# One of four weight units of a pair formed on GpSimd instead of VectorE

## The reference

```python
xn   = rms_norm(h, norm_pre_mix);  cols = xn @ w_in
# cols -> q, k, v | r, k, v and four decay/rate parts, gate | two merge gates
o_attn = banded_gqa_attention(q, k, v, sink)
o_rwkv = rwkv7_bidirectional(...)      # 32 heads of 64, a forward and a backward scan
mix  = (sigmoid(g_attn) * o_attn + sigmoid(g_rwkv) * o_rwkv) @ w_out
h    = h + rms_norm(mix, norm_post_mix)
h    = h + rms_norm(square(relu(rms_norm(h, norm_pre_ffn) @ w_ffn_up)) @ w_ffn_down, norm_post_ffn)
```

## Time and profile before

| | us |
|---|---|
| median of 3 runs | 2259.21 |
| lowest and highest | 2257.98, 2265.47 |
| profiled execution | 2251.1 |
| its span | 2249.3 |
| TensorE busy | 2097.0 (93%) |
| VectorE busy | 1312.6 (58%) |
| ScalarE busy | 926.4 (41%) |
| GpSimd busy | 357.3 (16%) |
| mean granted TensorE clock | 0.962 of full |

### The profile page before, as it was taken

The page is one execution under the profiler, slowest core; times in us unless marked ns, Lnnn a source line. Parts: engine busy times, 40 slices in busy tenths (PEclk is TensorE's granted clock), DMA queues, the critical chain, the costliest instruction groups (busy, mean ns, idle before and its releaser), DMA issues.

```text
span 2249.3 us, 39352 instructions
## 1 busy us (share of the span) xinstructions
PE 2097.0 (93%) x14475; PEld 1912.1 (85%) x14475; DVE 1312.6 (58%) x2229; ACT 926.4 (41%) x1670; POOL 357.3 (16%) x424
## 2 busy tenths in 40 slices
PE   6999997999999999999999887979999999999996
PEld 6999996988888888888888766769989889899894
DVE  4666466566676666666666633455555555555554
ACT  4555333444444444434444422344434334344342
POOL 0000001333333333333333320000000000000000
PEclk9999998999999999999999857989999999999998
DMA  7546655223322322232331303535665656656662
GB/s 201 147 134 165 176 143 137 73 71 81 80 67 75 80 78 60 78 80 62 80 80 43 118 0 112 160 104 186 187 187 186 184 181 181 185 185 183 187 186 93
DMA packets 415085, 281.25 MB, mean 125 GB/s; under 512 B 14042, under 2 KB 372668, under 8 KB 414012
## 3 DMA queue, kind: packets, MB, share of 16 engines
q1 hardware_dynamic: 414620, 277.43, 42.7%
q10 hardware_dynamic: 416, 3.15, 0.4%
HBM read 278.46 MB, written 2.10 MB: 125 GB/s over the span
## 4 chain that ended last, share of the span: by engine, by line
issue 54%; PE 28%; DVE 10%; POOL 4%; ACT 2%; DMA 0%; SPq 0%; DVEq 0%; POOLq 0%; ACTq 0%
PE bank L1384 6%; PE bank L1386 5%; PE bank L1385 5%; POOL CT L1330 2%; DVE wlo L776 2%; PE bank L1639 2%; PE bank L1654 1%; PE bank L1400 1%; PE bank L1401 1%; PE bank L1402 1%; DVE dec L1027 1%; POOL st L1308 1%; PE bank L1659 1%; DVE kh L1019 1%; PE bank L1456 1%
## 5 line engine op out<-in xcount | busy, mean ns | idle before, releaser
L1384 PE MATMUL bank<-xT,whi 128*128 128x256 f32 x2784 | 820.4, 295 | 9.0 <-DVE wlo L776 4.6
L1385 PE MATMUL bank<-xT,whi 128*128 128x256 f32 x2784 | 787.2, 283 | 0.0
L1386 PE MATMUL bank<-xT,wlo 128*128 128x256 f32 x2784 | 786.8, 283 | 0.0
L1384 PEld LDWEIGHTS bank<-xT,whi 128*128 128x128 f32 x2784 | 533.6, 192 | 16.3 <-issue 10.1
L1385 PEld LDWEIGHTS bank<-xT,whi 128*128 128x128 f32 x2784 | 533.8, 192 | 1.5
L1386 PEld LDWEIGHTS bank<-xT,wlo 128*128 128x128 f32 x2784 | 532.2, 191 | 0.0
L776 DVE TENSOR_TENSOR wlo<-raw,whi 128x1024 fp32r<-128x1024 f32 (+1 forms) x160 | 244.1, 1525 | 164.1 <-ACT whi L424 102.7
L1262 DVE TENSOR_TENSOR wlo<-raw,whi 128x1024 fp32r<-128x1024 f32 x126 | 154.4, 1226 | 201.1 <-ACT whi L743 201.1
L743 ACT ACTIVATE whi<-raw 128x1024 fp32r<-128x1024 f32 x126 | 133.0, 1055 | 218.1 <-PE bank L1402 218.1
L1401 PE MATMUL bank<-wlo,ft 128*128 128x512 f32 x512 | 202.2, 395 | 0.0
L1402 PE MATMUL bank<-whi,ft 128*128 128x512 f32 x512 | 202.2, 395 | 0.0
(11 more groups left out here) (214 smaller groups left out, 3267.6 us busy)
## 6 DMA issues: line engine op xcount, KB each, us to landing
raw<-in_w_in SPq DMA_DIRECT2D x106, 1024.0 KB, 6.0
raw<-in_w_ffn_up SPq DMA_DIRECT2D x64, 1024.0 KB, 6.3
raw<-in_w_ffn_down SPq DMA_DIRECT2D x64, 1024.0 KB, 5.0
raw<-in_w_out SPq DMA_DIRECT2D x16, 1024.0 KB, 5.0
raw<-in_w_in SPq DMA_DIRECT2D x4, 768.0 KB, 4.7
xtok<-in_x SPq DMA_DIRECT2D x2, 1024.0 KB, 5.8
upg<-in_g_up SPq DMA_DIRECT2D x16, 128.0 KB, 3.4
hres<-in_x ACTq DMA_DIRECT2D x1, 2048.0 KB, 9.3
```

What stands on the lines that cost most here:

```text
L1384: M(bank[:, 0:T], h, xT[:, k, 0, :], start=k == 0, stop=False)
L1385: M(bank[:, 0:T], h, xT[:, k, 1, :], start=False, stop=False)
L1386: x = M(bank[:, 0:T], l, xT[:, k, 0, :], start=False, stop=k == KT - 1)
```

## The change

POOL now forms the gate unit's low part: behind its level-0 and level-1 masks of both d, ahead of the level-2 masks. It waits for `w_hi` of that unit, does both halves one after the other, and counts `w_lo`. DVE's two halves are gone. Since POOL and DVE now both count `w_lo`, DVE waits for POOL's count before its next cut (of the next unit, after level 4). Nothing changes for the other three units of a pair, for ACT, PE or SP.

```diff
@@ dve, pair
                 nx = Prep(n) if n is not None else None
-                cut_pair(1, d1, 0)
 
                 for l in range(1, LV):
@@
-                        if l == 1 and d == 0:
-                            cut_pair(1, d1, 1)
+                        if l == 4 and d == 1 and d1 is not None:
+                            dve.wait_ge(w_lo.sem, w_lo.n(4 * d1 + U_RW + 4))
                         if l in (4, 5) and d == 1:
                             cut_pair(2, d1, l - 4)
@@ pool
-            def pair(i, n):
+            def pair(i, n, d1):
@@
                     level(1, d)
+                if d1 is not None:
+                    u = U_RW + 3
+                    pool.wait_ge(w_hi.sem, w_hi.n(4 * d1 + u + 1))
+                    for part in (slice(0, 1024), slice(1024, 2048)):
+                        x = Gp.tensor_tensor(wlo[:, u % 2, part], raw[:, u % 4, part], whi[:, u % 2, part].bitcast(f32), ALU.subtract)
+                    x.then_inc(w_lo.sem, 1)
                 for l in range(2, LV):
                     for d in range(2):
                         w("wmm", 2 * (l - 2) + d + 1)
@@
             with pool.Fori(0, PAIRS - 1, 1) as i:
-                pair(i, i + 1)
-            pair(PAIRS - 1, None)
+                pair(i, i + 1, i + 1)
+            pair(PAIRS - 1, None, None)
```

## The result

The changed kernel took 2366.46 us (median, 2360.81 to 2370.87) against 2258.60 us (2252.42 to 2265.47): a ratio of 1.0477, 95% interval 1.0445 to 1.051. The direction was forecast; the size, 108 us where 58 were expected, lies outside the range of 2292 to 2337. The profiled execution took 2369.6 us with a span of 2367.8, which is 118.5 us over the span of before.

The account below looks back on a forecast made before the run. PE's in-order program was taken to set the pace. 15 pairs x 2.8 = 42 us of net stall plus 16 us of clock falls made 58 us; 2259.2 + 58 = 2317 us, range 2292 to 2337.

Parts of the forecast that it names:

- What bounds the kernel: PE, in order and busy 57.22 of 60 us in a steady pair, sets the pace; its stalls are paid in full.
- cover: At level 2, d = 0, POOL's CT mask is ready about 2 us before PE's product needs it.
- POOL's price: Each 1024-column half of the subtraction on POOL takes 2.28 us, between 2.16 and 2.40, from its smaller operations.
- rival 2: POOL slower than its small operations say, by contention or two float32 streams: 2336 to 2365 us; chance 0.15.
- The stall and the relief: PE idles 3.18 us before the level-2 product; DVE's lighter queue and faster AS copies return 0.4; net 2.8 a pair.
- Rival 3: The subtraction hides ahead of the level-2 masks, at 0.7 us a half or less: 2253 us, not slower; chance 0.02.
- The clock: The new PE stall brings a clock fall in about 10 of 15 pairs, 1.6 us each: 16 us.
- the fall at 1004: Half clock over 1004 to 1008 in the earlier trace; that pair took 61.39 us against 59.80, pricing one fall at 1.6.
- the bound of 24 us: Upper bound of the clock's cost, with a fall in all 15 pairs.
- the 8 us that the sum carried over from profile to median: The runs' median lay 8 us above the profiled execution; this was kept, turning 2309 into 2317 us.
- the length of an idle stretch: PE idle 4.62 us was followed by half clock, 3.48 us near the start was not; the new stall is shorter.
- rival 1: The clock holds and only the stall is paid: 2301 us, or 2297 with 2.16 us a half; chance 0.28.

Follow-up runs that it names:

- half-and-half kernel: Changed kernel with POOL forming only the first 1024 columns of the gate unit's low part and DVE the second half: 2303.22 us, ratio 1.0175.
- both places filled: Changed kernel with seven zero products in PE's level-2 stall and three more among the Gram products: 2292.57 us, ratio 1.0166.
- the stall filled: Changed kernel with seven zero products of PE per pair just ahead of the level-2 product that waits for POOL: 2312.02 us, ratio 1.0215.

## Why the prediction was wrong

*What bounds the kernel.* Right: PE's order, and the masks of level 2 with a cover of about 2 us, of which 1.4 us were left once ACT's second half is waited for. POOL's share of 16% says nothing of this.

*POOL's price.* Right: 2.36 us a half against 2.28, inside 2.16 to 2.40; 1.27 us for 512 and 3.46 for 1536 columns lie on the same line, 0.18 + 0.55 for each 256. Contention (rival 2) did not come; VectorE has nothing with two SBUF inputs to do there, and in the half-and-half kernel, where it has, POOL's masks slowed down by 11% in the mean. (Rival 2's 2365 is a slip: 2346 and 16 are 2362.)

*The stall and the relief.* Right: 3.14 us against 3.18, and 2.81 net against 2.8. The relief that this implies is 0.33 us, where 0.4 was read from the rows; it was not isolated. No later part gave the stall back. Rival 3 (hidden in the cover) was rightly small: it took 512 columns to hide.

*The clock: the step that failed.* The text gave a fall 1.6 us and ten pairs, 16 us in all. The number was too low and the size much more so: 21 falls, of 8.6 us in the mean and so some 3.7 us each (8.6 x 0.43). The clock fell behind the stall in all 15 pairs, and among the Gram products in six places. And a fall is not of one size: those behind the stall lasted 3.4 to 13.7 us, 8 us in the mean. I took the price from the fall at 1004, which lasted 3.4 us, the shortest that occurs; the bound of 24 us rested on it too. With 0.43 us for each us at half clock, 180 us against 10 make 170 x 0.43 = 73 us; with 15 x 2.81 = 42 that is 115 of the 118.5 us between the spans. The remaining 3 us were not looked into. The medians lie 108 us apart and not 118, because the 8 us that the sum carried over from profile to median did not hold: the changed kernel's median is 3 us below its profiled execution.

The rows had a warning that I used for the chance but not for the size: at 1004 the clock fell though PE was busy 3.53 of 4 us. What makes a fall short or long is not shown: in the pair above PE reads as busy for all of 632 to 634, and the clock stays at 0.50.

The other reading that failed is that of the earlier trace rows, where the length of an idle stretch was taken as a sign of whether the clock falls. The same wait near the start, with the same program up to there, stands in all 13 profiled executions, 2.60 to 4.12 us long. The clock was at its lower level behind it in 11 of them; the two others are the kernel before (3.48 us) and the one with both places filled. PE's timeline and windows with the stall filled, then with both places filled:

```profile
26.17 0.58 PE L1389 MATMUL bank<-xT,whi 128*128 128x256 f32 x1 [2.72 <-DVE xT L811]
26.00:30.00 4.00, 3.83 (x20) 0.57 1.17 300
...
25.93 0.39 PE L1389 MATMUL bank<-xT,whi 128*128 128x256 f32 x1 [3.30 <-DVE xT L811]
26.00:30.00 4.00, 4.00 (x35) 1.00 1.18 299
```

So 3.48 us without a fall was luck of one execution, and no sign for rival 1. The Trainium skill, TensorE: Matmul & The Clock Gate, Part 1, says that the window in which activity is looked at runs freely of the kernel. These executions agree (2.72 us brought a fall, 3.30 us did not), and so do the stalls of 1.9 us (14 pairs of 15) and 0.83 us (nine of 15); for the stall of 3.14 us the trace shows no pair without one.

*Rival 1* (the clock holds, 2301 us) was not what happened, but the kernel with both places filled is that case: 2292.6 us, or 2284 without the 8 us of its added products, an estimate.

## What to carry to other kernels

Work moved to an idle engine costs what it delays in that engine's own queue: compare its length with the time between the last input and the moment at which the next result is wanted, not with the engine's idle share. When the change opens a stall on TensorE, read how long the half clock lasts behind stalls of all kinds in the trace, and count both places: where the stall is, and other thin stretches that it may tip over. When medians of small edits seem to contradict the account, compare the length of one repeated piece at full clock first, and the time at half clock separately.

## What the runs showed of the hardware

- Falls of the clock in the stage of the pairs lasted 3.4, 6.8, 10.2 or 13.7 us, and a us of them cost 0.36 (1024 columns) to 0.43 us (changed kernel) in this mix of work.
- An idle stretch of TensorE is not judged by its length alone: one wait near the start brought half clock at 2.60 us in one execution and not at 3.48 us in another.
- Between the pairs, among small float32 products with waits of 0.2 to 0.3 us, the clock fell although PE reads as busy 3.53 of 4 us. One product of zeros in the wait ahead of the fifth Gram product (seven of them took 3.18 us elsewhere) was enough that no fall was left there in the profiled execution (median 2250.91 us); two gave 2249.33 us. Which trait of the small products matters was not isolated.
- The scatter of the kernel before goes with its granted clock: its 55 runs beside the experiments spread over 2248 to 2269 us while their mean clock goes from 0.963 down to 0.953; the 22 runs with three zero products lie between 2250 and 2258 us. That it is falls between the pairs that come and go is likely, but only one execution of the kernel before was profiled.
- POOL's copy of `AS` took 1.42 us for two when VectorE had no operation with two SBUF inputs beside it, and 2.41 us when it had.
